# Attention gate products regrouped, GpSimd's decay product moved behind beta, and the first expert pair's gather split, in a hybrid encoder layer on one core

## The reference, cut to what matters

```python
h = rmsnorm(x, norm1_g) * (1 + sc1) + sh1                     # 512 tokens x 1024
q, k, v, feat, gl = split(h @ w_in)                            # 8 heads x 64, 2 kv heads; feat 1920; gl 2048
att = windowed_attention(q, k, v, sink) @ w_br_attn            # |t-s| <= 128, blocks of 128 queries
rw  = rwkv7_bidir(feat, ...) @ w_br_rwkv                       # two scans, 8 heads x 64
g_att, g_rw = split(sigmoid(gl))
x = x + gt1 * ((g_att * att + g_rw * rw) @ w_out)
h = rmsnorm(x, norm2_g) * (1 + sc2) + sh2
aff = softmax(h @ router_w); gates, idx = top_k(aff.T, 64)     # 16 experts, 64 tokens each
hid = silu(h[idx] @ w_gate) * (h[idx] @ w_up)                  # 1024 -> 2048, per expert
x = x + gt2 * scatter_add((hid @ w_down) * gates)
out = rmsnorm(x, final_g)
```

## Time and profile before

| | |
|---|---|
| median of 3 runs | 1558.31 us (1557.33 to 1558.44) |
| the profiled execution | 1559.51 us |
| its span, first to last instruction | 1557.8 us |
| TensorE busy | 1395.8 us (90%), mean granted clock 0.97 |
| VectorE, ScalarE, GpSimd busy | 458.3, 218.5, 41.0 us |
| HBM read | 470.93 MB |

### The profile page before, as it was taken

The page is one execution under the profiler, slowest core; times in us unless marked ns, Lnnn a source line. Parts: engine busy times, 40 slices in busy tenths (PEclk is TensorE's granted clock), DMA queues, the critical chain, the costliest instruction groups (busy, mean ns, idle before and its releaser), DMA issues.

```text
span 1557.8 us, 21703 instructions
## 1 busy us (share of the span) xinstructions
PE 1395.8 (90%) x9315; PEld 658.1 (42%) x9315; DVE 458.3 (29%) x813; ACT 218.5 (14%) x444; POOL 41.0 (3%) x45
## 2 busy tenths in 40 slices
PE   5999999899799995999889889889889889889888
PEld 1444444445676644453243343343343243243232
DVE  2799745751236425101101101201100201200102
ACT  2035003331321111110010010010010010010002
POOL 2002130000000000000000000000000000000000
PEclk9999999999899996999999999999999999999999
DMA  9953142261303447799999999999999999999996
GB/s 350 368 179 102 55 109 81 81 176 56 138 4 144 151 209 282 307 428 428 428 428 429 429 428 429 428 429 429 428 428 429 428 429 429 428 429 429 427 426 252
DMA packets 91844, 485.52 MB, mean 312 GB/s; under 512 B 36140, under 2 KB 53630, under 8 KB 62470
## 3 DMA queue, kind: packets, MB, share of 16 engines
q1 hardware_dynamic: 91725, 484.59, 76.5%
q10 hardware_dynamic: 56, 0.01, 0.0%
HBM read 470.93 MB, written 10.50 MB: 309 GB/s over the span
## 4 chain that ended last, share of the span: by engine, by line
PE 56%; DMA 30%; DVE 9%; issue 2%; ACT 2%; SPq 1%; DVEq 0%; ACTq 0%; PEldq 0%
PE psum L1161 14%; DMA arena<-in_exp_w_up_dram 14%; DMA arena<-in_exp_w_gate_dram 13%; PE psum L1178 9%; PE psum L680 7%; PE psum L1139 4%; DMA arena<-in_ada_w_dram 4%; PE psum L1071 4%; PE psum L592 2%; PE psum L994 2%; PE psum L1267 1%; PE psum L1198 1%; DVE arena L1674 1%; DVE arena L1579 1%; PE psum L758 1%
## 5 line engine op out<-in xcount | busy, mean ns | idle before, releaser
L1161 PE MATMUL psum<-arena 128*64 128x512 f32 x2048 | 469.5, 615 | 84.2 <-DMA arena<-in_exp_w_up_dram 45.5
L1161 PEld LDWEIGHTS psum<-arena 128*64 128x64 f32 x2048 | 164.4, 141 | 382.4 <-issue 382.1
L1178 PE MATMUL psum<-arena 128*64 128x512 f32 x960 | 209.2, 593 | 8.1 <-issue 6.3
L592 PE MATMUL psum<-arena 128*128 128x512 f32 x336 | 147.4, 599 | 1.4 <-DVE arena L1605 1.4
L1178 PEld LDWEIGHTS psum<-arena 128*64 128x64 f32 x960 | 80.6, 137 | 131.0 <-issue 130.8
L680 PE MATMUL psum<-arena 128*128 128x512 f32 x256 | 122.3, 610 | 0.0
L592 PEld LDWEIGHTS psum<-arena 128*128 128x128 f32 x336 | 63.8, 192 | 82.3 <-issue 79.5
L1982 DVE TENSOR_TENSOR arena<-arena,psum 128x512 f32<-128x512 f32 x32 | 19.8, 683 | 266.9 <-PE psum L1161 266.9
L1996 DVE TENSOR_TENSOR arena<-psum,arena 128x1024 f32<-128x1024 f32 x7 | 8.6, 1225 | 253.1 <-PE psum L1178 253.1
L1507 ACT ACTIVATE arena<-psum,arena 128x128 f32<-128x128 f32 x64 | 24.3, 457 | 325.7 <-PE psum L1139 325.7
L1974 DVE TENSOR_TENSOR arena<-arena,psum 128x512 f32<-128x512 f32 x32 | 19.8, 683 | 168.3 <-ACT arena L1516 168.3
(11 more groups left out here) (282 smaller groups left out, 1115.8 us busy)
## 6 DMA issues: line engine op xcount, KB each, us to landing
arena<-in_exp_w_gate_dram SPq DMA_DIRECT2D x64, 2048.0 KB, 25.2
arena<-in_exp_w_up_dram SPq DMA_DIRECT2D x62, 2048.0 KB, 26.8
arena<-in_exp_w_down_dram SPq DMA_DIRECT2D x60, 2048.0 KB, 27.0
arena<-in_ada_w_dram SPq DMA_DIRECT2D x24, 1024.0 KB, 10.0
arena<-in_w_in_dram SPq DMA_DIRECT2D x16, 1024.0 KB, 5.7
arena<-in_exp_w_down_dram SPq DMA_DIRECT2D x8, 1024.0 KB, 27.0
arena<-in_x_dram SPq DMA_DIRECT2D x2, 2048.0 KB, 8.4
gate_pre<-arena SPq DMA_DIRECT2D x16, 256.0 KB, 5.9
```

The costliest lines, as they stand in the source:

```text
L592: ins = mm(bank(b % 4), by(w_ring[g % 2], KC)[:, k, j * P:(j + 1) * P], by(hT, KC)[:, k, :], start=(k == 0), stop=(k == KC - 1))
L1161: ins = mm(bank(4 * kind + n)[e * 64:(e + 1) * 64, :], by(xeT, KC)[:, k, e * 64:(e + 1) * 64], by(ring[(j + e) % RING], 2)[:, r, n * 512:( ...
L1178: ins = mm(bank(4 + n)[e * 64:(e + 1) * 64, :], by(hidT, FBLK)[:, 4 * kk + b, e * 64:(e + 1) * 64], by(ring[(j + e) % RING], 4)[:, b, n * ...
```

## The change

1. GpSimd waits for `beta_ready` ahead of `KD * LC`.
2. The gate products of the attention stand otherwise. q = 0: 1 behind each pair of scores (before 2), 10 ahead (before 6), then 4, 2, 2, 2 (before 3, 3, 2, 2). q = 1 and 2: 2 behind each pair, 8 ahead (before 6), then 4, 2, 2, 2: 26 products in the place of 24. q = 3: as before, with the last 20. The four behind the attention are gone from there. On ScalarE `gate_out(1)` goes behind the second exponential of q = 0.
3. The first pair's gather is issued as groups 0 to 2, gate chunk couple 0, groups 3 to 5, couple 1, groups 6 and 7, couples 2 and 3. In the loop `widen(i, 0, 1..3)` moves from the start of the body to its end, for the next pair; the work of TensorE is in the same order there, only the branch back stands elsewhere.

```diff
@@ gpsimd
             pool.wait_ge(sem("exps_done"), 3)
+            pool.wait_ge(sem("beta_ready"), 1)
             s(nc.gpsimd.tensor_tensor(KD, KD, LC, ALU.mult))
@@ tensor, attention
-                g0 = 8 + 24 * q
-                ahead, doubled = ((6, 2), (6, 2), (6, 2), (4, 0))[q]
+                g0 = (8, 32, 58, 84)[q]
+                each, ahead, first = ((1, 10, 4), (2, 8, 4), (2, 8, 4), (2, 4, 2))[q]
...
-                    gate_products(g0 + 2 * j, g0 + 2 * j + 2)
-                gate_products(g0 + 8, g0 + 8 + ahead)
-                g0 += 8 + ahead
+                    gate_products(g0, g0 + each)
+                    g0 += each
+                gate_products(g0, g0 + ahead)
+                g0 += ahead
...
-                    more = (3 if k < doubled else 2)
+                    more = 2 if k else first
...
-            gate_products(100, 104)
@@ tensor, experts
+            def more_gate(i, kk):
+
+                pe.wait_ge(sem("xe_ready"), 4 * i + kk + 1)
+                widen(i, 0, kk)
+
             def pair(i, last):
 
-                for kk in range(1, 4):
-                    pe.wait_ge(sem("xe_ready"), 4 * i + kk + 1)
-                    widen(i, 0, kk)
...
+                for kk in range(1, 4):
+                    more_gate(i + 1, kk)
 
             gather(0, 4, 0, 3, 2)
             first_gate(0, True)
-            gather(0, 4, 3, KC, 2)
+            gather(0, 4, 3, 4, 2)
+            for kk in range(1, 4):
+                gather(0, 4, 2 * kk + 2, min(2 * kk + 4, KC), 2)
+                more_gate(0, kk)
@@ scalar
-                for idx in ((0, 1), (4,), (7,), (10,))[q]:
+                for idx in ((0,), (4,), (7,), (10,))[q]:
...
                     prob_exp(h)
+                    if q == 0 and h == 1:
+                        gate_out(1)
```

## The result

The changed kernel takes **1543.75 us** (median of 4 runs, 1542.86 to 1546.9), the kernel before 1558.38 us in the same rounds (4 runs, 1557.33 to 1560.46): a ratio of 0.9908 [0.9891, 0.9926], 14.6 us faster. The forecast was 1544.7. The profiled execution took 1544.05 us, with a span of 1542.3 us against 1557.8.

A forecast was written before the change was run, and what follows sets the result against it. The expert stage was taken as bound by its weight stream, which inherits gains ahead of it. Terms -2.6, -2.4, -6.7 and -1.9 sum to -13.6 us: 1545.9 for the profiled execution, 1544.7 predicted, range 1541.5 to 1551.5.

The forecast's parts named there:

- part 1, idle time: At the turn of the values: TensorE's wait for the last shift goes once GpSimd's product follows beta, -2.6 us.
- part 1, clock: At L661, behind that wait: 128 records at full clock take 3.05 us in place of 5.5, -2.4 us.
- part 2: Attention: regrouped gate products remove TensorE's waits and one group start, and the gain carries on to the stream, -6.7 us.
- part 3: Expert stage's start: couple 1 runs ahead of 8 gather matmuls, so the stream's hole ends earlier, -1.9 us.
- branch back: Expert loop on TensorE: moved between couple 3 and the up products, where it waits 2.66 us anyway, 0 us.
- Cover: GpSimd behind its delayed product: L528 waits for the last shift until 205.6, giving 20 us of cover.
- start: GpSimd's product `KD * LC` would start at 174.2 us, behind beta, and end at 185.0.
- the free shift: VectorE's next shift, reading PSUM beside GpSimd's product, costs 0; at worst it waits until 185.0, still 0.
- fits by hundredths: q = 2 of the attention: VectorE scales the last two heads at 317.52, TensorE asks at 317.4; 0.1 us charged.
- The queue: Stream start: 4 MB loaded at 640.4 last until 651, leaving 1.6 us of queue; 0.1 us of new hole allowed.
- The bound of 2.0: Part 3, first pair's gather: the gain lies between 0, if the stream's start-up eats it, and -2.0 us.
- clock that other stages win by falling otherwise: Other stages: clock gain counted, with the bounds of parts 2 and 3, only in the range's low end, 1541.5 us.

The follow-up runs named there:

- e4: Kernel before with only the expert loop's branch back moved, the first pair's gather left in one piece; 1558.67 us, ratio 0.9998.
- e1: Kernel before with only GpSimd's wait for `beta_ready` added; 1554.04 us against 1558.44, ratio 0.9965.
- e5: Changed kernel with TensorE waiting for one more shift (`shift_done` 12, not 11) ahead of L662; 1548.33 us, ratio 0.994 to the kernel before.
- e9: Changed kernel with one gather group in place of three between couples 0 and 1; 1545.33 us, ratio 0.9913 to the kernel before.
- e10: Changed kernel run again unchanged, same chip and rounds as the run with couple 1 earlier; 1544.4 us, ratio 0.9909 to the kernel before.
- e8: Changed kernel with GpSimd's first sum (L524) also held behind `beta_ready`; 1545.23 us, ratio 0.9921 to the kernel before.
- e6: Changed kernel with 6 gate products ahead and 6 in the first group in q = 1 and 2; 1547.58 us, ratio 0.9936 to the kernel before.
- e7: Changed kernel with gate-product groups of 3, 3, 2, 2 behind the transposes in q = 0 to 2; 1547.65 us, ratio 0.9938 to the kernel before.

## Why the prediction was right

| step | forecast | measured | where |
|---|---|---|---|
| part 1, idle time | -2.6 | -2.6 | wait ahead of L662 gone |
| part 1, clock | -2.4 | -1.55 | 5.50 to 3.95 us |
| part 2 | -6.7 | -7.34 | scores to `x_blocks` |
| part 3 | -1.9 | -1.65 in this pair, -1.8 over all | gather to last up couple |
| branch back | 0 | 0 | e4, 0.9998 |
| sum | -13.6 | -13.2 | |
| not foreseen | 0 | -3.0, +1.4, -0.7 | clock ahead of the gather, last couple, start |

**Part 1.** The cause was as read from two end times: VectorE waited for GpSimd, and e1 shows it alone. The Trainium skill, in "SBUF — State Buffer", section on who interferes with whom, says that a VectorE instruction with two SBUF inputs and a GpSimd instruction that reads SBUF exclude each other for their whole length. The numbers agree: 10.80 us against 2.29, and GpSimd's own product 10.76 against 8.85. Cover (23.75 us idle ahead of L529), start (173.0 for 174.2, of which 0.74 is an earlier start of the projection's five blocks) and the free shift all came as worked out. For the free shift the prediction names GpSimd's rows 2 beside VectorE's L1689 at 218.23; the GpSimd instructions that ran then are those of L533, from 215.29 to 224.42 in the trace before, and the argument holds with them. The one wrong term is the clock: "128 / 42 = 3.05 us at full clock". A window counts every record that touches it, and in one microsecond many cross an edge. Windows inside L662 of the changed kernel:

```profile
179.00:181.00 2.00, 2.00 (x76) 2.00 (x72) 1.34 (x2) 1.17 (x3) 2.00 (x1) 1.00 0.00 0
179.00:182.00 3.00, 3.00 (x111) 3.00 (x108) 1.34 (x2) 1.83 (x4) 2.89 (x1) 1.00 0.00 0
```

One microsecond shows 41, two show 76, three show 111: the rate is 35 a microsecond, and 128 / 35 = 3.66 us, plus the run-out of the last records, is close to the measured 3.95. The count of a short window was taken for a rate, and that made the term 0.85 us too large. e5 shows the mechanism itself.

**Part 2.** Left over are 1.2 us of waits where I put "under 1.3", and `x_blocks` begins at 340.33 for a forecast of 341.0, 0.74 of it by the earlier start of the five blocks: against that start it moved 11.55 us for a forecast of 11.7. The scaling in q = 2 that "fits by hundredths" did not quite fit: the last transposes begin at 309.93, 2.01 us after the start of the two products ahead of them, where it is 1.82 us in q = 1 (276.61 - 274.79). That is 0.19 us, for 0.1 charged, and no bracket shows it. The gain is 0.64 above the forecast, and, with the two more products of each block allowed for, it lies in q = 1 (3.45 us for 2.88) and q = 2 (3.19 for 2.98). Two terms were left out of the sum. The transposes of two heads that a wait had parted take 0.52 us each, and together 0.82: 0.22 us in each of q = 1 and q = 2. And where TensorE does not wait, the transposes begin 0.16 or 0.17 us before the record of the products ahead of them ends (265.72 for 257.04 + 8.85 = 265.89 in q = 1, 269.86 for 266.42 + 3.60 = 270.02); behind a wait they cannot. In q = 1 that makes 0.22 + 0.17 + 0.16 = 0.55 of the 0.57. These are readings of the rows; no run tried them by themselves.

**Part 3.** The hole became two microseconds shorter, and the stretch to the last couple 1.65 to 2.1. The queue held, though by less than the prediction says: 4 MB asked for at 640.4 last 9.8 us at 428 GB/s, to 650.2 and not to 651, which leaves 0.9 us of queue where it has 1.6 (and 2.8 where it has 3.6). From the start of couple 1 to that of couple 2 it is 9.09 us in the changed kernel, less than the 9.8 that the 4 MB last, and 10.98 in e9, more than that, and there the second hole is. The bound of 2.0 was in place. As a time of the whole kernel it is at the edge of what medians tell.

**What came beside it.** Between `x_blocks` and the gather nothing was changed, and the stretch is 3 us shorter. Most of it sits between the first and the last of the branches' 128x512 products (L994 before, L995 after): 94.4 us before, 92.1 after, 91.1 in e10. Windows over it, before and then e10:

```profile
407.00:502.00 95.00, 86.12 (x2451) 62.33 (x2452) 40.46 (x81) 25.49 (x49) 0.00 (x0) 0.96 0.13 42
```
```profile
394.00:486.00 92.00, 82.94 (x2485) 61.63 (x2478) 40.82 (x82) 25.79 (x50) 0.00 (x0) 1.00 0.13 44
```

TensorE's idle time is the same (8.88 and 9.06 us); the busy time is 3.2 us shorter, at a mean granted clock of 1.00 for 0.96. The four profiles with both gains whole (after, e8, e9, e10) stand at 262.1 to 263.5 us for `x_blocks` to gather, the three that give some of a gain back (e5, e6, e7) at 264.3 to 265.4, those with one gain at 264.6 and 264.7, and the three with neither at 265.9 to 266.1. In these twelve profiles it goes with the change, then; why it does is open. Against it stand 1.4 us at the last couple in the profile after, which e10 does not have, and the execution of before that was profiled, 1.1 us above its median. So the mechanisms were right one by one, and the closeness of the number is in part luck: the clock term 0.85 us too large and the attention 0.64 too small nearly cancel, and the terms measured come to 13.2 us. By the medians the other 1.4 us were in no term; the prediction names "clock that other stages win by falling otherwise" only in its range.

## What to carry to other kernels

Where VectorE and GpSimd both work on SBUF tensors, compare their end times: an instruction that ends just behind the other engine's and is several times as long as its twin has waited for it, and moving the one that nobody waits for is worth the idle time of the engine that sets the time, and the clock behind it if the rows show that it falls there. Filler for TensorE is best laid so that what another engine needs (the last product of a block, here) is finished ahead of the place where that engine turns to it, and enough stands behind to hide its work; count both engines there, in us. Take a rate from the whole group of instructions, or from the difference of two windows, not from the count of a short one, and before a stream is released earlier, count what is queued behind: e9 moved the hole instead of closing it.

## What the runs showed of the hardware

- GpSimd's product of 128x4096 takes 8.85 us behind beta and took 10.76 beside VectorE's products of two SBUF tensors. It ended at 161.14, and 161.14 - 8.85 = 152.29 is about where VectorE's L1673 ended (152.46): it had waited as well. VectorE's L1673, 4.07 us, falls to 2.29 with GpSimd's sum out of the way (e8). The two took turns by whole instructions.
- A VectorE instruction that reads PSUM keeps its 0.75 us beside that product (178.05 and 178.84 above).
- A pause of 2.07 us of TensorE, behind 34.60 us of the projection's products, was followed by a clock of 0.50 (e5). The waits of 1.53 us in q = 1 and of 1.73 us in q = 2 were not: the clock in 270 to 274 and in 306 to 312 of the kernel before is 1.00. In the expert stage about half of the waits of 1.9 to 3.2 us were followed by it (156 of 305 couples took 8.42 to 8.79 us for 7.09), and none of the 151 under 1.5 us.
- The backward branch of the expert loop on TensorE's side takes 0.08 to 0.24 us, at either place.
- The same program, profiled twice, differs by 0.9 us from `x_blocks` to the gather (262.97 and 262.09), with the same instructions and waits within 0.1 us in the attention. So where the clock falls there is not fixed by the program, and a difference under 1 us in one profile of that stage says nothing.
